# Second attention of a hybrid decoder: six rows of logits, and another order on four engines

## The reference

```python
def causal_attention_blocks(q, k, v):          # 16 heads, q and k of 96, v of 64
    lg = jnp.einsum('bhqd,bshd->bhqs', qc, k, preferred_element_type=jnp.float32) * scale
    lg = jnp.where(pos[None, :] <= tq[:, None], lg, -jnp.inf)
    p = jax.nn.softmax(lg, axis=-1).astype(v.dtype)
    return jnp.einsum('bhqs,bshd->bqhd', p, v)
...
return o.reshape(B, S, MLA_HEADS * MLA_V) @ w_out
```

## Time and profile before

| | |
|---|---|
| median of 3 runs | 1352.5 us |
| the profiled execution | 1350.3 us, of which its span is 1348.1 us |
| PE busy | 1274.8 us (95%) |
| DVE, ACT, POOL busy | 749.2, 634.1, 38.1 us |
| late steps 2 to 10, on PE | 416.60 to 482.26 us of the span |

### The profile page before, as it was taken

The page is one execution under the profiler, slowest core; times in us unless marked ns, Lnnn a source line. Parts: engine busy times, 40 slices in busy tenths (PEclk is TensorE's granted clock), DMA queues, the critical chain, the costliest instruction groups (busy, mean ns, idle before and its releaser), DMA issues.

```text
span 1348.1 us, 15897 instructions
## 1 busy us (share of the span) xinstructions
PE 1274.8 (95%) x6208; PEld 900.8 (67%) x6209; DVE 749.2 (56%) x933; ACT 634.1 (47%) x730; POOL 38.1 (3%) x48
## 2 busy tenths in 40 slices
PE   7987999999886789999999999999999999999997
PEld 6765788888774668565856656766747574838472
DVE  5876454453585348464727555735646553837470
ACT  5575553453366346353625444535535443626350
POOL 1012000000001200000000000000000000000000
PEclk9999999999996889999999999999999999999999
DMA  9632455364361267799999999999999999999996
GB/s 338 221 127 82 137 187 188 123 229 151 101 216 67 94 272 264 302 393 404 421 421 421 421 418 417 420 422 419 422 418 417 420 421 421 421 419 417 420 421 257
DMA packets 88756, 422.92 MB, mean 314 GB/s; under 512 B 8560, under 2 KB 15462, under 8 KB 57958
## 3 DMA queue, kind: packets, MB, share of 16 engines
q1 hardware_dynamic: 87468, 419.10, 78.8%
q0 software_dynamic: 992, 2.69, 0.6%
q10 hardware_dynamic: 218, 0.08, 0.0%
HBM read 420.77 MB, written 1.07 MB: 313 GB/s over the span
## 4 chain that ended last, share of the span: by engine, by line
PE 84%; DVE 7%; ACT 3%; DMA 3%; issue 2%; SPq 0%; DVEq 0%; ACTq 0%
PE PS L2179 13%; PE PS L2155 11%; PE PS L2159 11%; PE PS L2156 11%; PE PS L1708 7%; PE PS L2171 7%; PE PS L1709 7%; PE PS L1712 7%; DMA raw<-in_w_down_o_dram 2%; PE PS L2186 1%; DVE w_r L974 1%; PE PS L2095 1%; PE PS L2104 1%; PE PS L1783 1%; ACT w_r L491 1%
## 5 line engine op out<-in xcount | busy, mean ns | idle before, releaser
L1388 DVE TENSOR_TENSOR w_r<-raw,w_r 128x2048 fp32r<-128x2048 f32 (+1 forms) x150 | 314.7, 2101 | 181.5 <-ACT w_r L802 181.0
L802 ACT ACTIVATE w_r<-raw 128x2048 fp32r<-128x2048 f32 (+1 forms) x150 | 264.9, 1766 | 201.7 <-PE PS L2159 118.7
L2155 PE MATMUL PS<-w_r,a_hi 128*128 128x512 f32 x512 | 201.8, 394 | 0.0
L2156 PE MATMUL PS<-w_r,a_lo 128*128 128x512 f32 x512 | 199.9, 390 | 0.0
L2179 PE MATMUL PS<-raw,xs 128*64 128x512 f32 (+1 forms) x856 | 169.9, 543 | 0.0
L974 DVE TENSOR_TENSOR w_r<-raw,w_r 128x2048 fp32r<-128x2048 f32 (+4 forms) x69 | 139.3, 2044 | 42.0 <-ACT w_r L491 41.7
L1708 PE MATMUL PS<-w_r,a_hi 128*128 128x512 f32 (+4 forms) x384 | 147.0, 387 | 6.8 <-DVE a_lo L1003 6.2
L1709 PE MATMUL PS<-w_r,a_lo 128*128 128x512 f32 (+4 forms) x384 | 142.5, 375 | 0.0
L491 ACT ACTIVATE w_r<-raw 128x2048 fp32r<-128x2048 f32 (+4 forms) x69 | 115.2, 1720 | 26.5 <-PE PS L1712 23.7
L2179 PEld LDWEIGHTS PS<-raw,xs 128*64 128x64 f32 x856 | 58.8, 137 | 92.8 <-issue 84.2
L2155 PEld LDWEIGHTS PS<-w_r,a_hi 128*128 128x128 f32 x512 | 96.2, 188 | 28.0 <-issue 8.5
(11 more groups left out here) (300 smaller groups left out, 1441.6 us busy)
## 6 DMA issues: line engine op xcount, KB each, us to landing
raw<-in_w_down_o_dram SPq DMA_DIRECT2D x94, 1024.0 KB, 18.6
raw<-in_w_gate_o_dram SPq DMA_DIRECT2D x53, 1024.0 KB, 14.4
raw<-in_w_up_o_dram SPq DMA_DIRECT2D x51, 1024.0 KB, 15.0
raw<-in_w_gate_o_dram SPq DMA_DIRECT2D x53, 768.0 KB, 12.4
raw<-in_w_up_o_dram SPq DMA_DIRECT2D x53, 768.0 KB, 12.2
slots<-in_w_down_o_dram SPq DMA_DIRECT2D x18, 1024.0 KB, 18.0
raw<-in_w_in_e_dram SPq DMA_DIRECT2D x12, 1024.0 KB, 10.3
raw<-in_w_down_e_dram SPq DMA_DIRECT2D x11, 1024.0 KB, 4.9
```

Source lines behind the costliest of these rows:

```text
L802: nc.scalar.activation(w_r[:, high_slot(g), 0:w], place_of(n)[:, 0:w], ACT.Copy).then_inc(hi_done, 1)
L1388: nc.vector.tensor_tensor(place_r(n)[:, 0:w], place_of(n)[:, 0:w], w_r[:, high_slot(g), 0:w], ALU.subtract).then_inc(lo_done, 1)
L2155: nc.tensor.matmul(PS[:, bank, :], xh(x), hi[:, c0:c0 + NT], start=first, stop=False)
L2156: nc.tensor.matmul(PS[:, bank, :], xl(x), hi[:, c0:c0 + NT], start=False, stop=False)
```

## The change

`lg1` gets six rows (LG1 = 6), so DVE may write the logits of head h once head h-6 has been turned. On ACT a late step now copies both turned heads first and takes both heads' exponentials after that. On PE the turn of the second head moves from the end of the step to the place between the two pieces of the projection. On DVE the order of a step becomes low part of pair s-3, norm of pair s-1, logits of pair s, where it was logits, norm, low part. The three splits of weights come one step later or more. The first attention keeps its four rows and its order. The work itself, instruction by instruction, is the same.

```diff
-        lg1, z1 = place(z0 + 2 * TT * GH * ROPE, "lg1", [P, 4, LOG])
+        lg1, z1 = place(z0 + 2 * TT * GH * ROPE, "lg1", [P, LG1, LOG])
...
+        def logits_of(h):
+            return lg[:, h % 4, :] if h < NH else lg1[:, (h - NH) % LG1, :]
...  ScalarE, late_step
-                for r in range(2):
-                    if 2 <= s < NH // 2 + 2:
+                if 2 <= s < NH // 2 + 2:
+                    for r in range(2):
                         probs_turned(NH + 2 * s - 4 + r)
-                    if s < NH // 2:
+                if s < NH // 2:
+                    for r in range(2):
                         head_exp(NH + 2 * s + r)
...
-            split_to(C_OUTO + 2)
             late_step(2)
             late_step(3)
+            split_to(C_OUTO + 2)
+            late_step(4)
             split_to(C_OUTO + 3)
-            late_step(4)
+            late_step(5)
+            late_step(6)
             split_to(C_OUTO + 4)
-            for s in range(5, NH // 2 + 2):
+            for s in range(7, NH // 2 + 2):
                 late_step(s)
...  VectorE, pair_logits
-                    if h >= 4:
-                        dve.wait_ge(sem("at_tr"), h - 3)
+                    if h - h0 >= deep:
+                        dve.wait_ge(sem("at_tr"), h - deep + 1)
...
+            pair_norm(0, NH)
             pair_logits(1, NH)
-            pair_norm(0, NH)
-            split_to(C_OUTO + 2)
+            pair_norm(1, NH)
             pair_logits(2, NH)
-            pair_norm(1, NH)
-            pair_logits(3, NH)
-            pair_norm(2, NH)
-            pair_low(0, NH)
-            split_to(C_OUTO + 3)
...
-            for s in range(5, NH // 2):
-                pair_logits(s, NH)
+            for s in range(3, NH // 2 + 1):
+                pair_low(s - 3, NH)
                 pair_norm(s - 1, NH)
-                pair_low(s - 3, NH)
-            pair_norm(NH // 2 - 1, NH)
-            pair_low(NH // 2 - 3, NH)
+                if s < NH // 2:
+                    pair_logits(s, NH)
+                if s in (3, 4, 6):
+                    split_to(C_OUTO + {3: 2, 4: 3, 6: 4}[s])
             split_to(C_MOE)
             pair_low(NH // 2 - 2, NH)
...  TensorE, late_step
+                if 2 <= s < NH // 2 + 2:
+                    head_turn(NH + 2 * s - 3)
                 if s >= 5:
                     out_piece(1, s - 5)
-                if 2 <= s < NH // 2 + 2:
-                    head_turn(NH + 2 * s - 3)
```

More of the change, by code:

```diff
@@ L71 @@
 GROUPS = 4
+LG1 = 6
 GH = NH // GROUPS
@@ L542, in head_exp @@
             def head_exp(h):
-                logits = lg if h < NH else lg1
+                logits = logits_of(h)
                 act.wait_ge(sem("at_max"), h + 1)
-                nc.scalar.activation(logits[:, h % 4, 0:P], logits[:, h % 4, 0:P], ACT.Exp,
+                nc.scalar.activation(logits[:, 0:P], logits[:, 0:P], ACT.Exp,
                                      bias=nm[:, h, 0:1], accum_out=rs[:, h, 0:1]).then_inc(sem("at_exp"), 1)
-                nc.scalar.activation(logits[:, h % 4, P:LOG], logits[:, h % 4, P:LOG], ACT.Exp,
+                nc.scalar.activation(logits[:, P:LOG], logits[:, P:LOG], ACT.Exp,
                                      bias=nm[:, h, 1:2], accum_out=rs[:, h, 1:2]).then_inc(sem("at_exp"), 1)
@@ L1048, in pair_logits @@
                         for t, (a, b) in enumerate(((0, P), (P, LOG))):
-                            out, top = logits[:, h % 4, a:b], nm[:, h, 2 + t:3 + t]
+                            out, top = logits[:, a:b], nm[:, h, 2 + t:3 + t]
                             ins = nc.vector.tensor_tensor_reduce(out, out, dmask[:, a:b], 1.0, TAKEN, ALU.add, ALU.max, top)
@@ L1054, in pair_norm @@
             def pair_norm(s, h0=0):
-                logits = lg1 if h0 else lg
                 for h in (h0 + 2 * s, h0 + 2 * s + 1):
+                    logits = logits_of(h)
                     dve.wait_ge(sem("at_exp"), 2 * h + 2)
@@ L1060, in pair_norm @@
                     dve.wait_ge(sem("at_rcp"), h + 1)
-                    nc.vector.tensor_scalar(logits[:, h % 4, 0:P], logits[:, h % 4, 0:P], rs[:, h, 2:3], None, ALU.mult)\
+                    nc.vector.tensor_scalar(logits[:, 0:P], logits[:, 0:P], rs[:, h, 2:3], None, ALU.mult)\
                         .then_inc(sem("at_norm0"), 1)
@@ L1670, in _, with heads @@
         def _(pool):
-            def heads(h0, n, logits):
+            def heads(h0, n):
                 for h in range(h0, h0 + n):
                     pool.wait_ge(sem("at_rcp"), h + 1)
-                    nc.gpsimd.tensor_scalar(logits[:, h % 4, P:LOG], logits[:, h % 4, P:LOG], rs[:, h, 3:4], None,
+                    nc.gpsimd.tensor_scalar(logits_of(h)[:, P:LOG], logits_of(h)[:, P:LOG], rs[:, h, 3:4], None,
                                             ALU.mult).then_inc(sem("at_norm"), 1)
@@ L1692, in _ @@
             pool.dma_start(gate_bias[:, :], b_router.to_broadcast([P, NE])).then_inc(sem("bias8_in"), 16)
-            heads(0, NH, lg)
+            heads(0, NH)
             pool.wait_ge(sem("resid"), 4)
@@ L1697, in _ @@
             pool.dma_start(gbc[:, 1, :], mla_k_norm[:, 64:QKD].to_broadcast([P, ROPE])).then_inc(sem("gbc_in"), 16)
-            heads(NH, 4, lg1)
+            heads(NH, 4)
             pool.wait_ge(sem("grp_tr"), NH)
             pool.dma_start(ffg[:, :], ffn_norm_o.to_broadcast([P, D])).then_inc(sem("ffg_in"), 16)
-            heads(NH + 4, NH - 4, lg1)
+            heads(NH + 4, NH - 4)
         @block.tensor
@@ L1780, in head_turn @@
                     pe.wait_ge(sem("at_pt"), h)
-                logits = lg if h < NH else lg1
                 for k in range(3):
-                    ins = nc.tensor.transpose(PS[:, 6, k * P:(k + 1) * P], logits[:, h % 4, k * P:(k + 1) * P], ident)
+                    ins = nc.tensor.transpose(PS[:, 6, k * P:(k + 1) * P], logits_of(h)[:, k * P:(k + 1) * P], ident)
                 ins.then_inc(sem("at_tr"), 1)
```

9 lines of the change are left out of this document (3 added, 6 removed).

## The result

The change ran at **1336.64 us** (median of 4, 1335.16 to 1339.44) against 1353.18 (median of 4) for the kernel before: a ratio of 0.9877, 95% interval 0.9854 to 0.9900. The forecast was 1338.4 with a range of 1334.8 to 1344.0, and faster at 0.92. The profiled execution took 1335.37 us with a span of 1333.5.

What follows compares the result with a forecast made beforehand. PE bounds the kernel, losing time where it idles or runs slowly. Late steps: 39.0 work + 8.1 idling + 4.4 surcharge = 51.5 us, 14.1 less than 65.66, giving 1338.4 us; range 1334.8 to 1344.0.

Steps and rivals of the forecast that it cites:

- The loop: Late steps: turn, logits, norms, low part and mix close once per step; breaking it removes five 2.3 us waits, 11.4 us.
- The second turn, both copies first: Late steps: the second piece hides the copy in steps 5 to 9; steps 3 and 4 idle 0.58 us each, 1.2 together.
- Splits: PE waits caused by weight splits behind steps 3, 4 and 6: 1.5, 3.5 and 1.8 us.
- surcharge: Extra PE work time in the late steps from a low granted clock: 4.4 us forecast instead of 10.1.
- End: Last low part, behind the first expert chunk's split: PE waits about 0.1 us instead of 0.60.
- Clock: Late steps: low from soon behind 418 to 425 us, costing 2.9, plus one later low stretch of about 1.5 us.
- The 866 us behind move as a block: Everything after the late steps, behind 482.26 us, keeps its length and only starts earlier.
- DVE and POOL in each other's way: Rival: logits stall under POOL's 1.91 us, steps 4 to 7 each about 1 us late; 1342.4 us, chance 0.06.
- Gain lost further on: Rival: expert weights then come late, so the gain does not reach the end; 1352.5 us, chance 0.05.
- Slower through a low clock: Rival: the clock stays low through all late steps, 12.3 us more; 1364.8 us, chance 0.02.
- as before: Rival: the clock falls as often as before in the late steps, surcharge 10.1 us; 1341.4 us, chance 0.20.
- none: Rival: the clock stays high, with no low stretch in the late steps; 1335 to 1337 us with its milder case, chance 0.15.

Runs made afterwards that it cites:

- experiment 9: The changed kernel with four rows and the three old orders of PE, ScalarE and VectorE, later splits kept: 1348.94 us, ratio 0.9966.
- experiment 6: The kernel before with one edit, the second turn moved between the two pieces of the projection: 1342.85 us, ratio 0.9922.
- 7: The changed kernel with the three old orders of PE, ScalarE and VectorE, six rows and later splits kept: 1340.71 us, ratio 0.9905.
- experiment 2: The changed kernel with the second turn again behind both pieces of the projection: 1339.12 us, ratio 0.9897.
- experiment 1: The changed kernel with four rows of lg1 instead of six: 1336.72 us, ratio 0.9875.
- experiment 11: The kernel of experiment 5 with ScalarE's evacuation of group 3's last heads ahead of pair 1's exponentials: 1329.20 us, ratio 0.9824.
- 3: The changed kernel with ScalarE's old order, copy and exponentials head by head: 1338.94 us, ratio 0.9897.
- 4: The changed kernel with VectorE's old order, logits, norm, low part, six rows kept: 1339.83 us, ratio 0.9896.
- experiment 8: The kernel of experiment 5 with VectorE's splits one step later, directly behind the norms, while POOL normalises: 1337.86 us, ratio 0.9880.
- experiment 5: The changed kernel with ScalarE's splits between the copies and the exponentials of steps 3, 4 and 6: 1329.91 us, ratio 0.9829.
- 10: The kernel of experiment 5 with four rows instead of six: 1329.55 us, ratio 0.9826.

## Why the prediction was right, step by step

**The loop: right, and more than right.** The reading of the earlier trace rows as a loop through PE and DVE held: undoing all its cuts (experiment 9) brings back 11.4 us in five waits. But the text credited its end to rows and VectorE's order together. The runs show that one edit alone already gives about half of the 16.5 us or more: the early turn, which the forecast credited only with hiding a copy, 11.1 us (experiment 6), six rows among the old orders 8.2 (from 9 to 7). With the other edits made the same two are worth 2.5 (experiment 2) and 0.1 (experiment 1). The edits' prices do not add up. VectorE's new order as the only edit was not tried.

**The second turn, both copies first: right.** The mixes of steps 9 and 10 lost their wait of 0.6 us. Step 3 begins with 0.58 as forecast, step 4 with 0.78, and a wait of 0.75 in step 4, for a copy behind the split of step 3, was not forecast.

**Splits: two right, one replaced.** Behind step 3: 1.5 forecast, 1.51 measured. Behind step 6: 1.8 forecast, 1.28 measured (5.86 less 4.58). Behind step 4: 3.5 forecast, 0.72 measured in step 5, where PE worked at the low level and was late itself; the wait for the split that was named as a sign did not come. Where that step ran at 1.00, its idling was 2.76 (experiment 1) and 3.88 (experiment 2), around the forecast. So the term was sized for a fast PE while the surcharge beside it was sized for a slow one; in one step only one of the two is paid.

**End: right.** 0.1 forecast, none measured. **Idle in all:** 8.1 forecast, 5.60 measured; the 2.8 of step 5 are the miss.

**Clock: right in kind, wrong in place.** Experiment 11 ran the whole stretch at 1.00 with 39.89 us of work, experiment 2 with 40.30, so 39.0 was about 1 us too low: steps 2 to 4 took 9.9 us in experiment 11 where 9.1 were counted. The surcharge is then 43.06 - 39.89 = 3.2 where 4.4 was forecast, and 9.2 before. (Of the 4.4, the 1.5 taken from step 7 is 7.41 less 5.74, so 1.7 by its own row.) None of it was behind 418, where I kept a fall; all was in step 5. There the granted clock was 0.66, and a stretch under 0.7 stood among the signs of being wrong: that sign came, though the time was right.

**Sum.** 39.9 + 5.6 + 3.2 = 48.7 against 51.5. The stretch lies 1.3 below the 50 to 53 I named and 2.8 below the sum: 0.9 more work, 2.5 less idling, 1.2 less surcharge. Of the 2.8, 2.4 were given back at its two sides, which the forecast held fixed. So the mechanism was right, and that the profiled execution came within 0.8 us of the forecast (1335.37 against 1336.2) is in part luck, errors that offset each other. **"The 866 us behind move as a block"** was off by 1.3: 867.1 in the change. In the experiments it is 866.2 (3 and 4) to 868.4 (2), and 867.2 in experiment 6, which has before's splits and rows; so one profile of before, the shortest of all, does not show that the orders lengthen it. The start, 1.1 later, lies within the spread told of below. Both stay open as to cause.

**Rivals.** DVE and POOL in each other's way: refuted for logits (0.28 us under POOL), shown for splits (experiment 8), which in the change never run beside POOL's norms. The Trainium skill, "SBUF — State Buffer", section "SBUF: two separate sides", draws the line just there: an operation that reads two SBUF inputs and a GpSimd operation exclude each other. By that rule whichever starts first holds the ports; here the GpSimd operation did the waiting and the split, which began during one, did not show its 0.4 us. Gain lost further on: refuted, 1.3 of 17. Slower through a low clock: refuted. Of the two on the clock, the surcharge of 3.2 lies between "as before" and "none", and since a high clock in step 5 came with 2 to 3 us more idling there, it is not a loss that a better clock would simply give back.

## What to carry to other kernels

When waits of equal length recur once per step, look for the loop, and for the cheapest single cut of it; price further cuts only with the first one made, since they overlap. Then look at what stands in queue behind long operations that two engines do one after the other: moving ScalarE's part ahead of its exponentials took 6.7 us off the median, 4.0 of them seen in the stretch, with no instruction added. In a step that waits for another engine, idling of TensorE and its low clock stand in for each other: step 5 took 9.94 us at 0.66 with 0.72 of idling, and 9.19 and 10.17 at 1.00 with 2.76 and 3.88 (experiments 1 and 2). So do not add both for one step.

## What the runs showed of the hardware

- **Where the clock falls is not set by the waits alone.** Experiment 2 kept 1.00 through 10.65 us of idling in fourteen waits, one of 2.59. Experiment 5, with 2.04 us of idling, had this in steps 2 and 3, and experiment 11, with the same order from step 2 on, had 1.00 there (windows of 5, then of 11):

```profile
416.31:419.44 3.13, 2.55 (x15) 1.99 (x15) 1.53 (x10) 1.04 (x3) 0.35 (x1) 0.77 0.46 168
419.44:425.76 6.32, 5.54 (x22) 4.03 (x23) 2.81 (x15) 3.23 (x12) 1.90 (x2) 0.57 0.00 0
```

```profile
418.00:421.31 3.31, 2.38 (x14) 1.72 (x14) 1.96 (x12) 2.61 (x11) 2.20 (x3) 1.00 0.00 0
421.31:425.09 3.78, 3.00 (x23) 2.23 (x23) 2.09 (x12) 3.08 (x12) 1.43 (x3) 1.00 0.44 139
```

  The low stretch of 5 cost 42.59 - 39.89 = 2.7 us. The level just ahead does not tell the two apart either: in the 6 us before step 2 it was 0.64 in experiment 5, 0.74 in 11, and 0.63 in the change, which ran steps 2 to 4 at 1.00. What decides is open.
- **The start of the stretch moves by 4 us between profiles of kernels that are the same ahead of it**: 416.31 in experiment 5, 419.00 in 10, 420.38 in 8 (10 differs by its four rows). The granted clock differed on the way: from 100 to 200 and from 200 to 300 us it was 0.98 and 1.00 in experiment 5, 0.95 and 0.98 in 8.
- **A weight split on VectorE, with both inputs in SBUF, holds up a GpSimd operation beside it** (2640 for 962 ns) and is not itself slowed (2275 to 2278 ns in three splits, 2293 alone in the change); the logits, with one input in PSUM, took 0.28 us under GpSimd's 1.91 and slowed neither.
